# Expert lists filled from the other end for odd experts, and 17 products on the identity ahead of the ranks in place of 26

## The reference

```
g_idx = argmax(x @ w_group + b_group)                 # 1 of 4 groups
top_v, top_i = top_k(e_logits of that group, 2)       # 2 of its 8 experts
expert = g_idx * 8 + top_i
h = silu(xb @ w_e_gate[e]) * (xb @ w_e_up[e])         # xb: the rows of one expert
y = h @ w_e_down[e]                                   # summed back to its token, weighted
```

## Time and profile before

| | us |
|---|---|
| median of 3 runs (lowest, highest) | 1267.2 (1266.77, 1269.09) |
| the profiled execution's own time | 1266.69 |
| its span, first to last instruction | 1264.9 |
| PE busy | 1231.1 |
| DVE busy | 656.4 |
| granted TensorE clock, mean | 0.997 |

### The profile page before, as it was taken

How to read it: one execution, slowest core, us unless ns; L and a number is a source line. 1 busy time by engine, 2 the same in 40 slices (tenths; PEclk the granted TensorE clock), 3 DMA queues, 4 the chain that set the end, 5 groups by cost and what they waited for, 6 DMA issues and landing times.

```text
span 1264.9 us, 16298 instructions
## 1 busy us (share of the span) xinstructions
PE 1231.1 (97%) x6164; PEld 826.8 (65%) x6164; DVE 656.4 (52%) x944; ACT 422.6 (33%) x610; POOL 61.0 (5%) x68
## 2 busy tenths in 40 slices
PE   6999999999999999999999999999999999998897
PEld 5888888888888888888888887333343343333332
DVE  5587765336365346337434755344454444444445
ACT  4778773223342333333343412211111111111114
POOL 0000000000000000000005200100000000000000
PEclk9999999999999999999999999999999999999998
DMA  7333322362323223223223599899999999999994
GB/s 236 108 86 96 98 70 82 95 181 87 98 67 100 83 67 99 84 82 90 79 75 101 186 402 380 360 410 408 417 414 413 413 415 418 411 416 418 413 422 167
DMA packets 143418, 286.05 MB, mean 226 GB/s; under 512 B 11781, under 2 KB 109173, under 8 KB 118784
## 3 DMA queue, kind: packets, MB, share of 16 engines
q1 hardware_dynamic: 139664, 276.81, 58.5%
q0 software_dynamic: 2544, 4.25, 1.0%
q10 hardware_dynamic: 1152, 4.19, 0.9%
HBM read 284.91 MB, written 4.33 MB: 229 GB/s over the span
## 4 chain that ended last, share of the span: by engine, by line
PE 84%; DMA 12%; DVE 2%; ACT 1%; issue 1%; SPq 0%; DVEq 0%; ACTq 0%
PE bank L1454 18%; PE bank L1455 18%; PE bank L1456 18%; PE bank L1753 13%; DMA m_raw<-in_w_e_up_dram 11%; PE bank L1785 6%; PE bank L1809 4%; PE bank L1743 1%; DVE wo_lo L894 1%; PE bank L1516 1%; PE bank L1778 1%; PE bank L1849 1%; PE bank L1696 1%; PE bank L1585 1%; PE bank L1508 0%
## 5 line engine op out<-in xcount | busy, mean ns | idle before, releaser
L1753 PE MATMUL bank<-m_raw,xe 128*64 128x512 f32 x1024 | 233.4, 598 | 12.4 <-DMA m_raw<-in_w_e_up_dram 12.3
L894 DVE TENSOR_TENSOR w_lo<-raw,w_hi 128x1024 fp32r<-128x1024 f32 x120 | 148.2, 1238 | 175.8 <-ACT w_hi L568 174.6
L1454 PE MATMUL bank<-xt_hi,w_hi 128*128 128x512 f32 x576 | 225.5, 392 | 1.1 <-DVE w_lo L894 1.1
L1456 PE MATMUL bank<-xt_hi,w_lo 128*128 128x512 f32 x576 | 224.4, 390 | 0.0
L1455 PE MATMUL bank<-xt_lo,w_hi 128*128 128x512 f32 x576 | 224.4, 390 | 0.0
L890 DVE TENSOR_TENSOR x<-x,bank 128x1024 f32<-128x1024 f32 x120 | 141.1, 1218 | 100.4 <-PE bank L1809 99.5
L568 ACT ACTIVATE w_hi<-raw 128x1024 fp32r<-128x1024 f32 x120 | 125.9, 1056 | 161.8 <-PE bank L1456 158.9
L1753 PEld LDWEIGHTS bank<-m_raw,xe 128*64 128x64 f32 x1024 | 71.6, 136 | 133.8 <-issue 132.3
L1454 PEld LDWEIGHTS bank<-xt_hi,w_hi 128*128 128x128 f32 x576 | 108.2, 188 | 24.8 <-issue 1.4
L1456 PEld LDWEIGHTS bank<-xt_hi,w_lo 128*128 128x128 f32 x576 | 108.2, 188 | 22.5
L1455 PEld LDWEIGHTS bank<-xt_lo,w_hi 128*128 128x128 f32 x576 | 108.2, 188 | 21.9
(11 more groups left out here) (276 smaller groups left out, 1653.3 us busy)
## 6 DMA issues: line engine op xcount, KB each, us to landing
m_raw<-in_w_e_gate_dram SPq DMA_DIRECT2D x64, 1024.0 KB, 27.1
m_raw<-in_w_e_up_dram SPq DMA_DIRECT2D x64, 1024.0 KB, 27.4
m_raw<-in_w_e_down_dram SPq DMA_DIRECT2D x64, 1024.0 KB, 27.1
raw<-in_w_in_dram SPq DMA_DIRECT2D x88, 512.0 KB, 3.8
raw<-in_w_ret_o_dram SPq DMA_DIRECT2D x16, 512.0 KB, 3.3
raw<-in_w_lru_o_dram SPq DMA_DIRECT2D x16, 384.0 KB, 3.2
raw<-in_w_out_dram SPq DMA_DIRECT2D x8, 512.0 KB, 3.9
x_rows<-in_x_dram ACTq DMA_DIRECT2D x4, 512.0 KB, 5.4
```

The lines of the kernel that those rows point to most:

```text
L894: return dve.tensor_tensor(dst, a, b_r.bitcast(F32), ALU.subtract)
L1454: pe.matmul(dst, sh, mh, start=first and x == 0, stop=False)
L1456: ins = pe.matmul(dst, sl, mh, start=False, stop=last and x == n - 1)
L1753: last = pe.matmul(bank[side:side + ROWS, 0, :], xe[:, 4 * half + k, :], w[:, FE * k:FE * k + FE], start=half == 0 and k == 0, stop=half = ...
```

## The change

Two tables of 32 numbers are added: `sign_e` is 1 for even and -1 for odd experts, `off_e` is 0 for even and 63 for odd ones. Rank times sign plus offset gives row r for even experts and 63 - r for odd ones. An odd expert with n rows so fills the rows 63 down to 64 - n of its list, and its gather writes the upper partitions of `xg`. The addresses of the overflow lists still need the plain ranks, so the sum over `prod` is computed a second time, after the lists are out. The idle products ahead of the ranks go from 26 to 17.

```diff
+            pool.iota(sign_e[:, :], pattern=[[0, EXPERTS // 2], [-2, 2]], base=1, channel_multiplier=0, allow_small_or_imprecise_dtypes=True)
+            pool.iota(off_e[:, :], pattern=[[0, EXPERTS // 2], [ROWS - 1, 2]], base=0, channel_multiplier=0, allow_small_or_imprecise_dtypes=True)
...
+            m_rows = rank_r[:, :].rearrange("p (t e) -> p t e", t=TT)
+            step(tt(m_rows, ranks, per_expert(sign_e), ALU.mult))
+            step.wait()
+            step(tt(m_rows, m_rows, per_expert(off_e), ALU.add))
+            step.wait()
             for k in range(2):
                 step(tt(prod[:, TT * k:TT * k + TT, :], mem[:, TT * k:TT * k + TT, :],
-                        ranks, ALU.mult))
+                        m_rows, ALU.mult))
...
             step(dve.tensor_reduce(af[:, 8:16], prod[:, :, :], AX, ALU.add))
+            step.wait()
+            for k in range(2):
+                step(tt(prod[:, TT * k:TT * k + TT, :], mem[:, TT * k:TT * k + TT, :], ranks, ALU.mult))
+            step.wait()
+            step(dve.tensor_reduce(af[:, 0:8], prod[:, :, :], AX, ALU.add))
...
-            keep_warm(26)
+            keep_warm(17)
             pe.wait_ge(members_ok, 1)
```

More of the change, by code:

```diff
@@ L244, in layer @@
         hot_g, best8, idx8 = rt("hot_g", 16), rt("best8", 8 * TT), rt("idx8", 8 * TT, U32)
+        sign_e, off_e = rt("sign_e", EXPERTS), rt("off_e", EXPERTS)
         slot_i, red, res = rt("slot_i", 32, I32), rt("red", 4), rt("res", 64)
@@ L252, in layer @@
         prod, mem = at("prod", 132, [P, 2 * TT, 32]), at("mem", 133, [P, 2 * TT, 32])
+        rank_r = at("rank_r", 134, [P, TT * EXPERTS])
         over, over_r, over_s = at("over", 134, [P, OVER]), at("over_r", 135, [P, OVER]), at("over_s", 132, [P, OVER])
@@ L1312, in _, with per_expert @@
             exp_row = over_c[:, 0:32]
+            def per_expert(ap):
+                return ap[:, :].unsqueeze(1).to_broadcast([P, TT, EXPERTS])
+            m_rows = rank_r[:, :].rearrange("p (t e) -> p t e", t=TT)
[3 more added lines that the diff above has]
+            step.wait()
             for k in range(2):
                 step(tt(prod[:, TT * k:TT * k + TT, :], mem[:, TT * k:TT * k + TT, :],
-                        ranks, ALU.mult))
+                        m_rows, ALU.mult))
             step.wait()
```

## The result

The changed kernel takes 1270.55 us (median of 20 runs, 1267.96 to 1273.87), the kernel before 1267.62 beside it on the same chips (20 runs, 1265.82 to 1271.33). The ratio is 1.0020, 95% interval 1.0012 to 1.0027: 2.5 us slower, where 1263.5 had been forecast.

A forecast was written before the change was run, and what follows sets the result against it. The stream of expert matrices was taken to set the end, through its restart and its slowest DMA engine. 1266.69 - 1.4 (routing) - 2.0 (rows) = 1263.3, said as a median of 1263.5; own range 1262.0 to 1264.9, 8 in 10 from 1262.0 to 1266.3.

The forecast's parts named there:

- What bounds the kernel: The stream of expert matrices sets the end, up to 12.3 us that PE has in hand.
- The routing: Nine fewer idle products: ranks 1.5 us earlier, 0.1 of added DVE steps exposed, SP's restart of matrix transfers 1.4 earlier.
- the cover by `sel`: The `sel` products on PE, 3.65 us, hide most of the 0.6 us that two added DVE steps cost.
- The hole: DMA idle time between the 21 early transfers and the stream's restart, to shrink from 6.2 to 4.8 us.
- Rival 2: TensorE's clock falls in the gap opened by the shorter idle block: +3.2 us, 1269.9; chance 0.05.
- rival 3: Routing brings nothing because another wait ends where the idle products ended; rows still gain: 1264.7; chance 0.07.
- The rows: Filling odd experts' lists from 63 down balances the gathers' rows over 16 DMA engines: 2.0 us gained.
- The bound of 0.7: Worst end for the rows: 0.7 us lost to 3.3 rows of chance imbalance, if place doesn't fix the engine.
- r mod 16: Assumed rule that gathered row r goes to DMA engine r mod 16: fullest engine 76 rows before, at most 66 after.
- 2.7 of 3.2 us: At the stream's end, 3.2 us of mean engine emptying measured; counts under r mod 16 gave 2.7 of it.
- pairs of neighbours: Rejected rule that neighbouring rows share an engine: 88 rows on the fullest, giving 5.1 us against the measured 3.2.
- Rival 1: Rows bring nothing: engine doesn't follow place, or r and 63 - r share one; only routing gains: 1265.3; chance 0.25.

The follow-up runs named there:

- e1: Kernel before with only the idle products cut from 26 to 17, rows and DVE steps as before: 1265.85 us, ratio 0.9979.
- e8: As e3, but empty places also fetch token 511, so 64 rows a gather, 1984 in place of 1003: 1292.24 us, ratio 1.0181.
- e9: As e3, but places 0 to 47 of each gather fetch, empty ones reading token 511, last 16 fetching nothing: 1286.53 us, ratio 1.0155.
- e6: Changed kernel with every list, expert 0's too, filled upward from place 16: 1278.79 us, ratio 1.0089 to before.
- e10: On e6's lists, places 16 to 63 fetch 48 rows a gather, empty ones reading token 511: 1298.98 us, ratio 1.0232.
- e15: Lists as in e3, each gather fetches exactly places 16 to 47, empty ones reading token 511: 1272.53 us, ratio 1.0032.
- e16: Lists as in e3, each gather fetches exactly the 32 even places, empty ones reading token 511: 1268.06 us, ratio 0.9999.
- e13: Lists as in e3, each gather fetches exactly places 0 to 31, empty ones reading token 511: 1265.43 us, ratio 0.9972.
- e3: Changed kernel with neutral tables: 17 idle products and all added steps, every row in its old place: 1266.28 us, ratio 0.9986.
- e5: Changed kernel, but odd experts' rows stand in rising token order in the same places, 64 - n to 63: 1269.92 us, ratio 1.0019.
- e11: Lists in old places, gathers of 48 places only, written to partitions 16 to 63: 1275.31 us, ratio 1.0061 to before.
- e12: As e3, but gathers of 48 places only, written to partitions 0 to 47: 1275.50 us, ratio 1.0051.
- e7: Changed kernel, but lists fill upward from place 4 x (e mod 4), so 0, 4, 8 or 12: 1270.43 us, ratio 1.0019.
- e14: Lists as in e3, each gather fetches exactly places 32 to 63, empty ones reading token 511: 1270.84 us, ratio 1.0017.
- e4: The changed kernel measured once more beside e1 and e3 on the same chip: 1270.18 us, ratio 1.0013; profiled execution 1271.53 us.

## Why the prediction was wrong

**What bounds the kernel**: right. The end follows the stream, both parts reached it.

**The routing**: right. 1.5 us had been booked for the ranks and 1.4 for the restart, with 0.1 exposed on DVE; it came to 1.66 in the trace, with nothing exposed, and to 2.7 (1.5 to 3.8) in the runs of e1. `ids` ended at 785.37, 0.12 us before the lists' weights load: the cover by `sel` held. The second addresses took the booked 1.0 us (789.01 to 789.96) and stayed hidden. The hole shrank by 1.2 of 1.4 us. Rival 2 (the clock) and rival 3 (another wait) didn't come about: the clock is 1.00 in the windows of after from 776 to 800, and the routing gave its gain.

**The rows**: the failed step. "10 rows less on the slowest engine, times 0.20: 2.0 us", with a loss of 0.7 as the worst end. Measured was a loss of 3.4 to 4.3 us. Three things in that step were wrong.
- The price of a row was read as the time of its own packets, 0.20 us. It is 0.40 (e8), since the matrices' packets beside it slow down as well, and it isn't one number: e9's added rows cost 0.71.
- A row's price was taken as the same at every place. e6, e9 and e10, and e15 and e16 show that it isn't, and the change moves 16 of the 31 gathers away from place 0: 2.5 us more of engines around each of them in the traces. This turned the sign, for a dearer row alone would have made the balance worth more. The bound of 0.7 came from imbalance only, and no row of before spoke of the place, since all its gathers start at place 0; the range should have had room for what had not been seen.
- The engine as r mod 16 was the rule that fitted best, but 2.7 of 3.2 us was one number fitted by one guess; e16, e9 and e10 exclude it. By pairs of neighbours the imbalance before is 88 - 62.7 = 25 rows and after 3, so balance should have been worth more than I booked, and still the emptying at the end stayed 3 us long. That window didn't measure the imbalance of the rows: e8, with all engines at 124, empties for 3.6 us. Rival 1 had said that the 3.2 us could stem from a stagger of other origin, and in that it was right; its time of 1265.3 was wrong all the same.

Is there a gain from balance at all? e13, even and low, stands at 0.9972 against 0.9986 of e3: 1.8 us, near the forecast 2.0, but the intervals overlap, so it isn't shown.

The range failed with this step. By the four kernels on one chip: routing 2.7 gained, added steps 0.9 lost (e1 to e3, not told from zero), rows 3.4 lost, 1267.6 + 1.6 = 1269.2, beside the 1270.55 measured. The 4.3 from e3 to the twenty runs closes the gap to 0.5, but holds that result itself.

What stays open: why the place of the rows within a gather slows the matrices' packets. It isn't the order of tokens (e5), the number or source of the rows (e9 and e10), nor an imbalance of the engines (e9 and e10 empty alike; e6 leaves the counts as they were), and the partition is at most a small part of it (e11 and e12). The theory under which most of these runs were made, that empty places ahead of the rows cost, fits e6, e7, e10 and e15, but 16 of them (e15) cost no less than 32 (e14), and the trace of e14 shows no cost around its gathers. What the engines have to do with the distance of a list's start from 0 or 32 isn't shown. No view shows single engines, and no run separated the empty places from the rows.

## What to carry to other kernels

Split a change of two parts before believing its sum: here one line of it was worth 2.7 us and the rest, 4 us the other way, hid it. The price of a small transfer beside a full stream isn't its own packet time; it is what the whole stream loses, and here it took a run with more of them to measure it. And where every instance in a trace looks alike (all lists from place 0), the trace holds no evidence on what another shape costs, in either direction.

## What the runs showed that was not expected

- A gathered 4 KB row beside the full stream of 8 KB packets costs 0.40 us of a DMA engine on the average of 981 more (e8), 0.20 to 0.23 of it in its own packets, and 0.71 on the average of 485 more (e9).
- With 48 rows a gather, the same ones, the places 0 to 47 give 1286.53 us and 16 to 63 give 1298.98: 12 us over 31 gathers, 0.4 us each, by nothing but which places are empty.
- Gathers of 48 places are slower than gathers of 64 that fetch the same rows and have 16 empty places more: 1275.50 (e12) against 1266.28 (e3), with 6.0 us of emptying at the end in place of 2.1.
- In the middle of the stream there are stretches of some 20 us with less throughput at full share (after, windows of 20 us):

```profile
1140.00:1160.00 20.00, 17.39 (x96) 7.36 (x94) 8.90 (x9) 2.15 (x4) 0.94 (x1) 1.00 1.02 403
1160.00:1180.00 20.00, 17.26 (x80) 6.51 (x78) 6.55 (x7) 2.15 (x4) 0.94 (x1) 0.83 1.01 393
1180.00:1200.00 20.00, 19.83 (x112) 8.08 (x108) 9.99 (x11) 3.34 (x6) 1.87 (x2) 1.00 1.01 414
```

They stand at other places in other executions (e4: 393 GB/s from 860 to 880 us and 378 from 920 to 940), so a single profile can't settle a question of 3 us: e14's profiled execution took 1266.28 us, 4.6 below its median of 12.

- The clock fell where the prediction had not looked. In the profiled execution of after, windows:

```profile
1158.00:1166.00 8.00, 8.00 (x48) 3.37 (x44) 3.57 (x5) 1.19 (x2) 0.94 (x1) 1.00 1.02 368
1166.00:1170.00 4.00, 1.26 (x8) 0.65 (x8) 0.75 (x1) 0.96 (x2) 0.00 (x0) 0.83 1.01 354
1170.00:1175.00 5.00, 5.00 (x14) 1.58 (x12) 0.00 (x0) 0.00 (x0) 0.00 (x0) 0.50 1.00 424
1177.00:1182.00 5.00, 5.00 (x31) 2.12 (x30) 2.65 (x3) 0.59 (x1) 0.00 (x0) 1.00 1.00 419
```

PE had run without a gap, then stood still for most of four microseconds while the stream was at its slowest (354 and 368 GB/s), and its granted clock fell from 1.00 to 0.50, from 2.4 to 1.2 GHz, until after 1175; by 1177 it is back. The end didn't hang on it: the chain of waits passes the slow stretch with a transfer, not with PE (start, us, what):

```profile
1168.83 32.02 DMA m_raw<-in_w_e_up_dram
```
